# Latent attention's projections with tokens in the partitions, its norms by one factor per token, and the LayerNorm output turned tile by tile

## What is computed

```python
def mla_mixer(xn, cos, sin, w_down, q_norm, kv_norm, w_uq, w_ukv, qn_norm, qr_norm, kn_norm, kr_norm, w_o):
    c = xn @ w_down                                     # 1024 -> 384 + 256 + 64
    q = (rms_norm(c[..., :384], q_norm) @ w_uq).reshape(1, 256, 8, 192)
    kv = (rms_norm(c[..., 384:640], kv_norm) @ w_ukv).reshape(1, 256, 8, 256)
    q_nope = rms_norm(q[..., :128], qn_norm)
    q_rope = apply_rope(rms_norm(q[..., 128:], qr_norm), cos, sin)
    k_nope = rms_norm(kv[..., :128], kn_norm); v = kv[..., 128:]
    k_rope = apply_rope(rms_norm(c[..., 640:], kr_norm), cos, sin)   # one for all heads
    # causal softmax((q_nope k_nope' + q_rope k_rope') / sqrt(192)) v, then @ w_o
```

## Time and profile before

| | |
|---|---|
| median of 3 runs | 2444.24 us (2442.36 to 2445.59) |
| the profiled execution | 2444.77 us, of which the span from the first to the last instruction is 2442.1 us |
| TensorE busy | 2223.9 us (91%), mean granted clock 0.954 |
| VectorE, ScalarE busy | 1589.6 us (65%), 1199.7 us (49%) |
| latent attention stage | 1791.9 to 1962.7 us |

### The profile page before, as it was taken

The page is one execution under the profiler, slowest core; times in us unless marked ns, Lnnn a source line. Parts: engine busy times, 40 slices in busy tenths (PEclk is TensorE's granted clock), DMA queues, the critical chain, the costliest instruction groups (busy, mean ns, idle before and its releaser), DMA issues.

```text
span 2442.1 us, 29583 instructions
## 1 busy us (share of the span) xinstructions
PE 2223.9 (91%) x11242; PEld 1871.2 (77%) x11242; DVE 1589.6 (65%) x2084; ACT 1199.7 (49%) x1489; POOL 40.0 (2%) x41
## 2 busy tenths in 40 slices
PE   5479999997999999999899997699985899999999
PEld 5258887776977888777798887688874788888887
DVE  7976558888537556888765558755557554566554
ACT  3125446775453545777445444554443354444443
POOL 1220000000000000000000000000000000000000
PEclk9688999998998999999899999899997899999999
DMA  6023568997503557999456554355631156545663
GB/s 248 18 78 132 190 197 310 339 359 266 189 19 110 174 182 241 354 347 347 156 174 198 186 179 140 100 182 182 196 129 52 50 180 193 182 163 172 198 192 101
DMA packets 123164, 452.17 MB, mean 185 GB/s; under 512 B 13808, under 2 KB 13808, under 8 KB 122128
## 3 DMA queue, kind: packets, MB, share of 16 engines
q1 hardware_dynamic: 121680, 442.55, 53.7%
q0 software_dynamic: 1056, 6.95, 0.8%
q10 hardware_dynamic: 288, 0.80, 0.1%
HBM read 449.19 MB, written 1.05 MB: 184 GB/s over the span
## 4 chain that ended last, share of the span: by engine, by line
PE 78%; DVE 13%; ACT 3%; issue 2%; DMA 2%; POOL 1%; SPq 0%; ACTq 0%; DVEq 0%; POOLq 0%
PE bank L298 20%; PE bank L300 19%; PE bank L299 19%; DVE w_lo L274 4%; PE bank L291 4%; PE bank L292 4%; PE bank L293 4%; DMA raw<-in_stream 2%; ACT w_hi L267 1%; DVE scr L2256 1%; PE bank L583 1%; DVE scr L2240 1%; PE bank L1017 1%; DVE scr L1625 1%; PE bank L2066 0%
## 5 line engine op out<-in xcount | busy, mean ns | idle before, releaser
L274 DVE TENSOR_TENSOR w_lo<-raw,w_hi 128x1024 fp32r<-128x1024 f32 x840 | 1003.3, 1223 | 531.0 <-ACT w_hi L267 527.8
L267 ACT ACTIVATE w_hi<-raw 128x1024 fp32r<-128x1024 f32 x840 | 875.3, 1058 | 722.6 <-PE bank L300 541.5
L298 PE MATMUL bank<-w_hi,x_hi 128*128 128x512 f32 x1024 | 403.6, 394 | 4.8 <-DVE x_lo L493 4.8
L299 PE MATMUL bank<-w_lo,x_hi 128*128 128x512 f32 x1024 | 400.5, 391 | 0.0
L300 PE MATMUL bank<-w_hi,x_lo 128*128 128x512 f32 x1024 | 400.4, 391 | 0.0
L298 PE MATMUL bank<-w_hi,c_hi 128*128 128x512 f32 x872 | 344.0, 394 | 43.2 <-issue 21.1
L299 PE MATMUL bank<-w_lo,c_hi 128*128 128x512 f32 x872 | 341.9, 392 | 0.0
L300 PE MATMUL bank<-w_hi,c_lo 128*128 128x512 f32 x872 | 341.8, 392 | 0.0
L291 PE MATMUL bank<-x_hi,w_hi 128*128 128x256 f32 x792 | 227.8, 288 | 25.6 <-DVE w_lo L274 20.9
L298 PEld LDWEIGHTS bank<-w_hi,x_hi 128*128 128x128 f32 x1024 | 193.6, 189 | 44.8 <-issue 5.6
L298 PEld LDWEIGHTS bank<-w_hi,c_hi 128*128 128x128 f32 x872 | 165.2, 189 | 80.8 <-issue 46.5
(11 more groups left out here) (397 smaller groups left out, 2251.1 us busy)
## 6 DMA issues: line engine op xcount, KB each, us to landing
raw<-in_stream SPq DMA_DIRECT2D x840, 512.0 KB, 4.3
ln_rows<-in_ln POOLq DMA_DIRECT2D x4, 1024.0 KB, 5.0
scr<-in_xt SPq DMA_DIRECT2D x1, 1024.0 KB, 5.1
scr<-in_s POOLq DMA_DIRECT2D x1, 1024.0 KB, 12.2
x<-in_x POOLq DMA_DIRECT2D x1, 1024.0 KB, 17.1
out_x<-x SPq DMA_DIRECT2D x4, 256.0 KB, 2.8
par<-in_par ACTq DMA_DIRECT2D x1, 752.5 KB, 9.2
scr<-in_ple POOLq DMA_DIRECT2D x1, 512.0 KB, 9.3
```

The costliest lines, as they stand in the source:

```text
L267: nc.scalar.activation(w_hi[:, n % RING, :], raw[:, n % RING, :], ACT.Copy).then_inc(hi_done, 1)
L274: nc.vector.tensor_tensor(w_lo[:, n % RING, :], raw[:, n % RING, :], w_hi[:, n % RING, :].bitcast(F32), ALU.subtract).then_inc(lo_done, 1)
L298: nc.tensor.matmul(out, xh, hi, start=start, stop=False)
L299: nc.tensor.matmul(out, xh, lo, start=False, stop=False)
```

## The change

The latent attention gets tokens in the partitions from the down projection to the rope. The down projection is six tiles with `three_by_token` instead of seven with `three`, its 64 rope columns twice instead of four times; the stage has 23 tiles instead of 24. The factor of `x` is no longer spread: squares are summed along the free dimension by ScalarE's accumulator (3 sums for each token tile), and VectorE makes one factor per token and latent on 128x2x3 elements. The latents are scaled, turned by ten transposes, and split with their norm weight. The heads come in five groups (k0, k1, the rope part r, n0, n1: four heads of k or q, or all eight rope parts, in two banks, one for each token tile), then two of v. ScalarE squares each head of a group by itself, 48 instructions in all, each with its accumulator; VectorE makes the factors on 128x8 or 128x16 elements and multiplies once for each bank. The norm weights of the rope parts are multiplied into the tables of sine and cosine, those of q and k into the copies after the transposes (16 for k, 16 for q, 8 for the rope of q, 2 for that of k). The score product takes the rope part as one product over 64 rows. The tiles of the weight stream are split between these steps, three of them inside the attention.

After a LayerNorm, each of the four banks now holds four chunks of one token tile, the rounding and the rest follow bank by bank, the router's matmuls write to `Q[0]` and wait for each token tile by itself, and the two halves of the PLE gate change their banks. Of the diff, with what was removed in the latent attention left out:

```diff
-        return 8 * 7 + 3 * 12 + 2 * 16 + 8 * 8
+        return 8 * 6 + 3 * 12 + 2 * 16 + 8 * 8
...
+            if kind(st + 1) == "raw":
+                for tt in range(TT):
+                    for q in range(2):
+                        b = Q[2 * tt + q]
+                        before(pe, b)
+                        pe.wait_ge(dve_did["x"], dve_did.at("x", st, tt, q))
+                        for c in range(4):
+                            last = nc.tensor.transpose(b[:, c * P:(c + 1) * P], x[:, tt, (4 * q + c) * P:(4 * q + c + 1) * P], column("ident", 0, P))
+                        last.then_inc(pe_did["x turned"], pe_did.next("x turned", st, tt, q))
+                        after(b, ("dve", ("x_lo", st, tt, q)))
+                return
...
+            if nxt == "raw":
+                for tt in range(TT):
+                    for q in range(2):
+                        act.wait_ge(pe_did["x turned"], pe_did.at("x turned", st, tt, q))
+                        nc.scalar.activation(chunks_of(x_hi, tt, q), four(Q[2 * tt + q]), ACT.Copy).then_inc(
+                            act_did["x_hi"], act_did.next("x_hi", st, tt, q))
...
+            if nxt == "raw":
+                for tt in range(TT):
+                    for q in range(2):
+                        dve.wait_ge(act_did["x_hi"], act_did.at("x_hi", st, tt, q))
+                        nc.vector.tensor_tensor(chunks_of(x_lo, tt, q), four(Q[2 * tt + q]), chunks_of(x_hi, tt, q).bitcast(F32), ALU.subtract).then_inc(
+                            dve_did["x_lo"], dve_did.next("x_lo", st, tt, q))
+                return
...
+                if st and kind(st) == "raw":
+                    if k % 4 == 0:
+                        for tt in tiles:
+                            pe.wait_ge(dve_did["x_lo"], dve_did.at("x_lo", st - 1, tt, k // 4))
+                elif k % 2 == 0:
                     pe.wait_ge(dve_did["x_lo"], dve_did.at("x_lo", st - 1, k // 2))
             return ready
...
-            logits = Q[3][:, 0:2 * TT * N_EXPERTS].rearrange("p (t j e) -> p t j e", t=TT, j=2)
-            before(pe, Q[3])
+            logits = Q[0][:, 0:2 * TT * N_EXPERTS].rearrange("p (t j e) -> p t j e", t=TT, j=2)
+            before(pe, Q[0])
             pe.wait_ge(dve_did["start lo"], dve_did.at("start lo", "router"))
             for tt in range(TT):
                 for k in range(KC):
-                    if tt == 0:
-                        input_ready(pe, st)(k)
+                    input_ready(pe, st, [tt])(k)
                     nc.tensor.matmul(logits[:, tt, :, :], x_hi[:, k, tokens(tt)], rw[:, k, :, :], start=k == 0, stop=False, skip_group_check=True)
                     last = nc.tensor.matmul(logits[:, tt, 0, :], x_lo[:, k, tokens(tt)], rw[:, k, 0, :], start=False, stop=k == KC - 1,
...
+            for part, first, count in (("a", 0, 2), ("a", 2, 2), ("b", 0, 4), ("a", 4, 2), ("a", 6, 2), ("b", 4, 4)):
+                n = pe_at.block // BLOCKS_PER_TILE
+                pe_at.block += BLOCKS_PER_TILE
+                pe.wait_ge(lo_done, n + 1)
+                width = 4 * P if part == "a" else 2 * P
+                for tt in range(TT):
+                    out = (Q[tt] if part == "a" else Q[2 + tt])[:, 0:width]
+                    for j in range(count):
+                        k, cols = first + j, slice(j * width, (j + 1) * width)
+                        if tt == 0 and part == "a":
+                            ready(k)
+                        mm = three_by_token(out, x_hi[:, k, tokens(tt)], x_lo[:, k, tokens(tt)], (w_hi[:, n % RING, cols], w_lo[:, n % RING, cols]),
+                                            k == 0, k == KC - 1)
+                    tile = n if tt == TT - 1 else None
+                    if k == KC - 1:
+                        mm.then_inc(pe_did["down"], pe_did.next("down", st, part, tt, tile=tile))
...
+            for i in range(3):
+                before(pe, Y[i])
+            for tt in range(TT):
+                pe.wait_ge(act_did["latent q"], act_did.at("latent q", st, tt))
+                pe.wait_ge(dve_did["latent"], dve_did.at("latent", st, "kv", tt))
+                for c in range(5):
+                    last = nc.tensor.transpose(bank(Y[c // 2])[:, c % 2, tokens(tt)], latent[:, tt, c * P:(c + 1) * P], column("ident", 0, P))
+                    if tt == TT - 1 and (c % 2 or c == 4):
+                        last.then_inc(pe_did["latent turned"], pe_did.next("latent turned", st, c // 2))
+            for i in range(3):
...
+            def heads(g):
+                first, ks = GROUPS_OF_HEADS[g]
+                for k in range(ks):
+                    n, b = divmod(pe_at.block, BLOCKS_PER_TILE)
+                    pe_at.block += SLAB
+                    pe.wait_ge(lo_done, n + 1)
+                    c = first + k
+                    pe.wait_ge(dve_did["latent lo"], dve_did.at("latent lo", st, c // 2))
+                    for tt in range(TT):
+                        if k == 0:
+                            before(pe, head_bank(g, tt))
+                        mm = three_by_token(head_bank(g, tt)[:, :], c_hi[:, c, tokens(tt)], c_lo[:, c, tokens(tt)], slab_of(n, b), k == 0, k == ks - 1)
...
+            for g in ("k0", "k1", "r", "n0", "n1"):
+                heads(g)
+            turn_heads("k", k_rows, K_TURNED, "dve")
+            heads("v0")
+            heads("v1")
+            turn_heads("q", q_rows, Q_TURNED, "act")
+            turn_heads("r", qr_turned, R_TURNED, "act")
+            before(pe, psum[2])
+            pe.wait_ge(dve_did["rope"], dve_did.at("rope", st, "k"))
+            for tt in range(TT):
+                last = nc.tensor.transpose(psum[2][:, tokens(tt)], kr_turned[:, tt, :], column("ident", 0, P))
...
-                    for half in range(2):
-                        nc.tensor.matmul(out, m_qr[:, half, g, qs], m_kr[:, n % 4, half, ks_], start=False, stop=True, skip_group_check=True)
+                    nc.tensor.matmul(out, m_qr[rows, n // 2, qs], m_kr[rows, ks_], start=False, stop=True, skip_group_check=True)
...
+            for tt in range(TT):
+                act.wait_ge(pe_did["down"], pe_did.at("down", st, "a", tt))
+                nc.scalar.activation(m_sq[:, 0, 0:384], Q[tt][:, 0:384], ACT.Square, accum_out=latent_ss[:, tt, 0:1])
+                nc.scalar.activation(m_sq[:, 1, 0:ROPE], Q[tt][:, 384:384 + ROPE], ACT.Square, accum_out=latent_ss[:, tt, 2:3])
+                act.wait_ge(pe_did["down"], pe_did.at("down", st, "b", tt))
+                nc.scalar.activation(m_sq[:, 1, 256:512], Q[2 + tt][:, 0:256], ACT.Square, accum_out=latent_ss[:, tt, 1:2]).then_inc(
+                    act_did["latent squared"], act_did.next("latent squared", st, tt))
+                act.wait_ge(act_did["latent squared"], act_did.at("latent squared", st, tt))
...
+            for g in ("k0", "k1", "r", "n0", "n1"):
+                for tt in range(TT):
+                    act.wait_ge(pe_did["heads"], pe_did.at("heads", st, g, tt))
+                    sums = head_stat(head_ss, g, tt)
+                    src = heads_of(head_bank(g, tt), g)
+                    for j in range(src.shape[1]):
+                        last = nc.scalar.activation(m_sq[:, tt, j * src.shape[2]:(j + 1) * src.shape[2]], src[:, j, :], ACT.Square,
+                                                    accum_out=sums[:, j:j + 1])
+                last.then_inc(act_did["head squared"], act_did.next("head squared", st, g))
+                split_hi(act, 2 if g in ("r", "n1") else 1)
+                act.wait_ge(act_did["head squared"], act_did.at("head squared", st, g))
+                if g != "k0":
+                    name = "k" if g == "k1" else g
+                    at, n = HEAD_STATS[name]
+                    act.wait_ge(dve_did["head variance"], dve_did.at("head variance", st, name))
+                    rsqrt_act(act, head_var[:, at:at + n], head_r[:, at:at + n], ("head seed", st, name))
+            for g in ("v0", "v1"):
+                for tt in range(TT):
+                    act.wait_ge(pe_did["heads"], pe_did.at("heads", st, g, tt))
+                    half = int(g[1])
+                    nc.scalar.activation(m_v[:, tt, half_of(half)], head_bank(g, tt)[:, :], ACT.Copy).then_inc(
+                        act_did["turned copy"], act_did.next("turned copy", st, g, tt))
+                split_hi(act, 1)
+            for i in range(4):
...
+            r2 = latent_t[:, 0, 0:TT]
+            mul(r2, rstd_tok, rstd_tok)
+            dve.wait_ge(act_did["latent squared"], act_did.at("latent squared", st, 1))
+            mul(latent_var, latent_ss, column("inv_width", 0, 3).unsqueeze(1).to_broadcast([P, TT, 3]))
+            mul(latent_var, latent_var, r2.unsqueeze(2).to_broadcast([P, TT, 3]))
+            nc.vector.tensor_scalar(latent_var, latent_var, NORM_EPS, None, ALU.add).then_inc(
+                dve_did["latent variance"], dve_did.next("latent variance", st))
```

(57 more changed lines are left out.)

370 lines of the change are left out of this document (156 added, 214 removed).

## The result

The changed kernel takes 2407.97 us (median of 4 runs, 2403.68 to 2411.70) against 2443.30 (2438.99 to 2445.59): ratio 0.9857, 95% interval 0.9835 to 0.9879, 35.3 us less where 46.7 were forecast; 2398 was forecast, 10 us below what was measured. The profiled execution has 2408.37 us with a span of 2406.6. The stage of latent attention, from the first transpose of x at its start to that of the next stage, went from 170.8 us to 142.4, where the terms of the prediction gave 128.

The account below looks back on a forecast made before the run. TensorE, busy 91% of the span, bounds the kernel except in stretches like latent attention, where it waits for VectorE and ScalarE. Terms -3.4, -15.5, -23.2, -0.7, -3.9 sum to -46.7: 2444.8 to 2398 us (2393 to 2403; range 2386 to 2413).

Parts of the forecast that it names:

- down projection, from the transposes of x on: Start of the latent attention stage: fewer, wider matmuls on TensorE's path, 20.2 us to 16.8, so -3.4.
- projection to heads: Last down-projection matmul to first head product: much smaller factor operations, 23.0 us to 7.5, so -15.5.
- heads: Head products up to the attention: a chain through ScalarE's squares, weight tiles and VectorE, 72.6 us to 49.4, so -23.2.
- attention: Attention of eight heads: bound moves from TensorE to VectorE, 29.9 us to 29.2, so -0.7 (0 to -5).
- output product: Product behind the attention, wholly bound by TensorE: stays as it is, 0.
- LayerNorm part: After the LayerNorms: router starts 2.3 us earlier twice, stick-breaking attention 0.7 later; -3.9, between 0 and -5.
- rival (1): Heads: TensorE stays at 1.2 GHz and is the bound, heads 60 us, +11, total 2409; chance 0.20.
- four tiles of 12 matmuls of 512 and two of 24 of 256: Down projection: the matmul count after the change, priced at 16.8 us against 20.2 before.
- rival (4): Idle gaps in heads keep half clock through attention (46 us) and output product (+20); 2446, slower than before; chance 0.03.
- those stretches are dense and ran at 1.00: Attention and output product: the argument against half clock there, from the clock in the trace before.
- the dropped product of 384 columns is 0.67 a head: Attention scores: TensorE's saving from one product fewer, 0.67 us a head, 5.3 in all.
- rival (2): Shorter hand-overs and full clock: heads 45 us, latents 6.5, attention 26, total 2388; chance 0.13.

Follow-up runs that it names:

- e1: Changed kernel with its LayerNorm part put back as before, so only the latent attention stage is new; 2411.38 us.
- e7: Changed kernel with one of two weight tiles split ahead of the squares in the head groups that split two; 2399.80 us.
- e2: Changed kernel with the down projection adding into banks 4 to 7, which the turn of x does not use, and the latent turned into banks 0 to 2; 2403.16 us.
- e3: Changed kernel with 20 unread products of 128x512 on TensorE between the transposes of the queries and those of the rotated parts; 2401.13 us.
- e5: Changed kernel with VectorE's rotation of the queries' rope part moved ahead of the split of two weight tiles; 2401.80 us.
- e11: Changed kernel with the rotation ahead of the split and the scores' rope products on 128 rows with zeros; 2396.28 us.
- e9: Kernel of e8 with the edit of e7 added, one of two weight tiles split ahead of the squares; 2383.09 us.
- e8: Changed kernel with three edits: down projection in banks 4 to 7, rotation ahead of the split, rope products on 128 rows with zeros; 2389.05 us.
- e12: Kernel of e9 with VectorE forming each weight tile's low part one head later than ScalarE rounds it in the attention; 2380.93 us.
- e4: Changed kernel with the scores' rope products on 128 rows, unused rows holding other numbers of the rotated key by mistake; 2401.75 us.
- e6: Changed kernel with the scores' rope products on 128 rows, zeros in the unused rows; 2400.74 us.

## Why the prediction was right in sign and 10 us too low

By its own terms, forecast and measured (us; before from the earlier trace rows):

| term | forecast | measured | |
|---|---|---|---|
| down projection, from the transposes of x on | -3.4 | +0.8 | 23.5 to 24.3 |
| projection to heads | -15.5 | -15.2 | 23.0 to 7.8 |
| heads | -23.2 | -23.2 | 72.6 to 49.4 |
| attention | -0.7 | +9.0 | 29.9 to 38.9 |
| output product | 0 | 0 | |
| LayerNorm part | -3.9 | -3.4 | by the medians of e1 and the changed kernel |

The measured terms give -32.0 of the 35.3 us between the medians, 14.7 short of the forecast's 46.7. The other 3.3 lie outside the stage of latent attention and are scatter as far as is known: the three stages behind a LayerNorm last 997.5 us in the profile before, 991.2 in the changed kernel's, and 994.2 in that of e1, whose code is there that of before.

The time of 2407.97 lies outside the forecast of 2393 to 2403 and inside the range to 2413. The range went that far for rival (1), half clock in the heads. What made the kernel slower than forecast was a late start and half clock in the attention, so that the range holds it by luck.

**Projection to heads: right**, mechanism and size. **Heads: the sum was right**, and the chain that it followed is the one that e7 found. Its parts were less exact: a Square of 128 columns takes 0.25 us and one of 64 0.20, where I took 0.30 and 0.25 (48 x 0.05 = 2.4 us less), the longest wait for a weight tile was 3.6 instead of 4 to 6, and v1 waited 2.0 us for the copies of the keys. The clock was 0.88, not 0.76. So an exact total stands on errors that cancelled. Rival (1), half clock through the heads, came only in stretches: the first 5.5 us, 3.4 behind the longest wait, and the last 3.5.

**Down projection: the step that failed was its start.** "four tiles of 12 matmuls of 512 and two of 24 of 256", 16.8 us, was right to 0.1 (e2). But I counted only the matmuls and not what the first one waits for. The diff shows that the down projection now writes four banks, and `before` for all of Q was in the code; I had read the same effect for the router and the last bank, and priced it there. Cost 2.6 us, and 1.6 for the half clock behind the rest: together the 4.2 us missing in this row.

**Attention: two assumptions of the step failed.** The first is the clock: the step took 1.00 throughout, and against rival (4) it says that "those stretches are dense and ran at 1.00". Rival (4), which had a chance of 0.03, has this mechanism, and it came in part: not to the output product, but for 17.4 us. e3 shows the rest before it as the trigger: filled with products, it brings no fall, and then the 64-row products bring none either. What they do is keep a low clock down: 17.5 us in e5 against 3.6 in e11, and 12.4 to 17.5 in the five kernels with them against 3.6 to 5.3 in the four without where the clock fell. Whether transposes hold the clock less than products do, which the prediction left open, the runs do not settle: ahead of the scores 24 transposes and the rest make 5.4 us in e5, and the clock falls; in e9 24 transposes and two rests make 5.9, and it does not. Price: 38.9 - 33.2 = 5.7. The second is "the dropped product of 384 columns is 0.67 a head": the two rope products that replace four have 64 rows, and each of the four changes of row count costs about 0.2 us, so a head's scores got no shorter (2.5 us against 2.4 before). The bound did not move to VectorE, as the step had it; it stayed with TensorE. Price: 33.2 - 30.8 = 2.4. With both put right (e8, e9) the bound is VectorE, and the step's 29.2 us misses only three waits of 0.58 us for ScalarE's rounding ahead of its rests (e12). 5.7 + 2.4 + 1.6 is the whole 9.7.

**LayerNorm part: right.** The router starts 2.2 us earlier twice (4.82 and 4.70 us after the first transpose, from 6.98 and 6.99). Ahead of stick-breaking attention the first product comes 0.45 us later, for which I had 0.7.

The best kernel is the one of e12 or e9, 27 or 25 us below the changed one: 0.975 of the kernel before.

Two slips of the working change nothing in the sum. The 48 Squares cover ten banks of 512 columns and not twelve, so that large ones would be 5.3 us in place of 6.4. The terms of rival (2) give 2389.5 and not 2388.

## What to carry to other kernels

Before counting a stage's matmuls, ask which banks the first one takes and who still reads them: a start 2.6 us late also brought 1.6 us of half clock. A term that assumes the full clock needs a look at the rest just ahead of it (2.3 to 5.5 us here) and at whether its own products bring the clock back: products of half the rows among small ones did not for 12 to 17 us. When a product is cut from 128 to 64 rows, pad it with zeros instead if its neighbours have 128.

## What the runs showed of the hardware

- TensorE, without a pause, stayed at 1.2 GHz for 17.4 and 17.5 us behind the first score (changed kernel and e5; 12.4 in e7, where it had fallen 5 us before that score) with two 64-row products among every six of a head's scores. With 128-row ones, zeros in half of the rows or not, it was back after 5.3 us (e4, e6), 3.6 in e11 and 3.8 in e12. TensorE was busy throughout in all of them. At 1.00, the same 64-row products did not make it fall (e3).
- A change between 64 and 128 rows costs about 0.2 us: scores of one head with four changes took 2.5 us against 1.75 with none.
- A rest of 2.3 to 2.7 us ahead of the scores let the clock fall in e5, e11 and e12 and not in e8 (1.00 from the first score on). A rest of 1.8 to 2.05 us ahead of v1 did within 1 us of its end in nine of the thirteen kernels, and not in the changed one, e2, e7 and e9. No run tells what made the difference.
